# Sums for the modulation of a two-layer block: who makes them and when, on one Trainium2 core

## The reference, cut to what matters

```python
mod = jax.nn.silu(c) @ mod_w + mod_b
shift1, scale1, gate1, shift2, scale2, gate2 = [m[:, None, :] for m in jnp.split(mod, N_MOD, axis=-1)]
h = rms_norm(x, g_pre_mix) * (1 + scale1) + shift1
... # short convolution, stick-breaking attention, Mamba-2 scan, three gates, w_o
x = x + (gate1 * rms_norm(mix_out, g_post_mix)).astype(x.dtype)
h2 = rms_norm(x, g_pre_ffn) * (1 + scale2) + shift2
f = (jax.nn.silu(gt) * up) @ w_ffn_out
x = x + (gate2 * rms_norm(f, g_post_ffn)).astype(x.dtype)
```

## Time and profile before

| | before |
|---|---|
| median of 3 runs | 1602.61 us (1602.59 to 1605.82) |
| the profiled execution | 1604.25 us |
| its span, first to last instruction | 1602.5 us |
| mean granted clock of PE | 0.984 of full |
| busy: PE, DVE, ACT, POOL | 1531.8, 963.6, 672.4, 654.4 us |
| PE not busy in the span | 70.7 us |

### The profile page before, as it was taken

How to read it: one execution, slowest core, us unless ns; L and a number is a source line. 1 busy time by engine, 2 the same in 40 slices (tenths; PEclk the granted TensorE clock), 3 DMA queues, 4 the chain that set the end, 5 groups by cost and what they waited for, 6 DMA issues and landing times. The chain is left out here.

```text
span 1602.5 us, 23250 instructions
## 1 busy us (share of the span) xinstructions
PE 1531.8 (96%) x8908; PEld 1344.2 (84%) x8908; DVE 963.6 (60%) x1387; ACT 672.4 (42%) x1109; POOL 654.4 (41%) x535
## 2 busy tenths in 40 slices
PE   9999999989999999999999999199999999999998
PEld 8878887878888999988898887078888889999886
DVE  4342767447578777743568887045445888887423
ACT  6223444323544455422577673022225544445321
POOL 3871005741534222494206308888016356641000
PEclk9999999999999999999999999699999999999999
DMA  7532231423523333544231214335224234444331
GB/s 212 171 118 79 60 73 54 157 84 96 162 79 93 106 106 106 157 151 135 83 106 53 80 36 136 92 105 157 80 96 119 79 99 132 116 110 124 112 106 53
DMA packets 189620, 171.40 MB, mean 107 GB/s; under 512 B 20688, under 2 KB 162000, under 8 KB 189520
## 3 DMA queue, kind: packets, MB, share of 16 engines
q1 hardware_dynamic: 181456, 144.84, 30.3%
q0 software_dynamic: 8064, 25.20, 5.2%
HBM read 167.91 MB, written 2.10 MB: 106 GB/s over the span
## 5 line engine op out<-in xcount | busy, mean ns | idle before, releaser
L1566 DVE TENSOR_TENSOR w_lo<-raw,w_hi 128x2048 fp32r<-128x2048 f32 (+1 forms) x109 | 212.7, 1952 | 232.4 <-ACT w_hi L1084 232.3
L2275 PE MATMUL bank<-h_hi,w_hi 128*128 128x512 f32 (+1 forms) x800 | 310.0, 387 | 0.0
L2277 PE MATMUL bank<-h_hi,w_lo 128*128 128x512 f32 (+1 forms) x800 | 298.9, 374 | 0.0
L2276 PE MATMUL bank<-h_lo,w_hi 128*128 128x512 f32 (+1 forms) x800 | 298.7, 373 | 0.0
L1084 ACT CAST w_hi<-raw 128x2048 fp32r<-128x2048 f32 (+1 forms) x108 | 171.5, 1588 | 197.4 <-PE bank L2277 191.8
L951 POOL TENSOR_SCALAR mod_raw<-mod_raw,c_silu 128x512 f32<-128x512 f32 x96 | 193.2, 2012 | 21.7 <-DMA mod_raw<-in_mod_w 17.9
L2275 PEld LDWEIGHTS bank<-h_hi,w_hi 128*128 128x128 f32 x800 | 151.4, 189 | 29.3 <-issue 1.9
L2276 PEld LDWEIGHTS bank<-h_lo,w_hi 128*128 128x128 f32 x800 | 151.2, 189 | 27.2 <-issue 1.9
L2277 PEld LDWEIGHTS bank<-h_hi,w_lo 128*128 128x128 f32 x800 | 151.0, 189 | 27.4
L2369 PE MATMUL bank<-s_hi,w_hi 128*128 128x256 f32 x576 | 165.4, 287 | 8.7 <-DVE act_m L1808 6.9
L2370 PE MATMUL bank<-s_lo,w_hi 128*128 128x256 f32 x576 | 162.9, 283 | 0.0
(11 more groups left out here) (476 smaller groups left out, 3320.5 us busy)
## 6 DMA issues: line engine op xcount, KB each, us to landing
raw<-in_w_in SPq DMA_DIRECT2D x102, 512.0 KB, 4.6
mod_raw<-in_mod_w POOLq DMA_DIRECT2D x96, 256.0 KB, 3.1
raw<-in_w_ffn_in SPq DMA_DIRECT2D x44, 512.0 KB, 5.0
raw<-in_w_gate SPq DMA_DIRECT2D x22, 512.0 KB, 4.1
raw<-in_w_up SPq DMA_DIRECT2D x22, 512.0 KB, 5.3
raw<-in_w_down SPq DMA_DIRECT2D x20, 512.0 KB, 4.5
raw<-in_w_ffn_out SPq DMA_DIRECT2D x20, 512.0 KB, 4.4
raw<-in_w_out SPq DMA_DIRECT2D x8, 512.0 KB, 4.4
```

The source lines that it names most:

```text
L1566: ins = dve.tensor_tensor(w_lo[s][:, cols], raw[s][:, cols], w_hi[s][:, cols].bitcast(F32), ALU.subtract)
L2275: pe.matmul(o, st_hi, mv_hi, start=first, stop=False)
L2276: pe.matmul(o, st_hi, mv_lo, start=False, stop=False)
L2277: return pe.matmul(o, st_lo, mv_hi, start=False, stop=last)
```

## The change

1. **Four pairs by DVE in the first units.** Pairs 0, 1, 3 and 5 (`EARLY`) are summed beside q, k and va. GpSimd clears one of two accumulators (`mod_both`), loads the bias and issues slabs of 1 MB (256 rows by 1024 columns, 4 a pair, 16 in all) into two buffers that lie in `x_in`. DVE multiplies and adds in one instruction, `scalar_tensor_tensor` of 128x1024, two to a slab (`early_slab`). PE's `mod_columns` of the four stand behind the k units and inside the va units. gate2 (pair 5) becomes a column too; GpSimd later multiplies the identity by it, so that `mod_gate` can spread it.
2. **Two pairs stay** (`LATER`: 2 and 4) with GpSimd, unchanged in form (`mod_pair`). The steps of pairs 1, 3 and 5 vanish from GpSimd's order, and `mod_columns` from the end of up and from merge; the gains are scaled by one small DVE instruction (`scale_gain`).
3. **All input sums on DVE:** S3 moves from GpSimd to DVE, ahead of the first tile. The rests of the plain tiles (`tile_lo`) and `split(n0 + 3)` are put in another order on DVE and ACT.
4. **T3 by GpSimd,** with T2 and T4: `t3_part` leaves DVE, and GpSimd makes T3 as soon as the weights are in and p7 of the block before is done.

The core of the diff, first the places and GpSimd's part:

```diff
+        mod_both = [mod_raw, mod_acc]
+        mod_slabs = [at(f"mod_slabs{s}", A + 32 + 8 * s, [P, 2, 1024]) for s in range(2)]
+        EARLY, LATER = [0, 1, 3, 5], [2, 4]
+        SLABS = KD // 2
...
+            def early_pairs():
+                for e, pair in enumerate(EARLY):
+                    acc, col = mod_both[e % 2], 512 * MOD_PAIRS[pair][0]
+                    wait(gp, mod_read, e - 1)
+                    then(gp.memset(acc[:], 0.0))
+                    gp.dma_start(acc[0:1, :, :].rearrange("p a n -> p (a n)"), a["mod_b_2"][:, col:col + 1024]).then_inc(mod_b_in, 16)
+                    for d in range(SLABS):
+                        slab = SLABS * e + d
+                        wait(gp, mod_summed, slab - 1)
+                        gp.dma_start(mod_slabs[slab % 2][:], mod_w2[:, 2 * d:2 * d + 2, col:col + 1024]).then_inc(mod_w_in[slab % 2], 16)
...
-            def blocks(n0, which, c, pair, done):
-                s3 = s_sum[:, S3]
-                gp.wait_ge(h_lo_done, 2 * KD * (c + 1))
...
+            def blocks(n0, which):
                 for m in range(BLOCKS):
                     n = n0 + PLAIN + m
+                    t3, t2, t4 = four(operand(w_sum, n0, 2)), four(operand(w_sum, n0, 3)), four(t4_sum(n0, m))
+                    gp.wait_ge(raw_in[UNITS[n]["slot"]], UNITS[n]["raw"])
+                    wait_operand_free(gp, n0, which, m, 2)
+                    gp.tensor_tensor(t3, quarter_of(n, 1, 1), quarter_of(n, 0, 1), ALU.subtract).then_inc(block_pool, 1)
...
-                    if 1 <= m <= 2 * KD - done:
-                        mod_step(pair, done + m - 1)
             gp.wait_ge(c_ready, 1)
-            mod_pair(0)
+            gp.wait_ge(xn_b_ready, NT)
+            early_pairs()
+            gp.wait_ge(mod_read, 3)
...
-            mod_begin(1)
-            for i in range(9):
-                mod_step(1, i)
             for t in range(NT):
                 gp.wait_ge(var_ready, t + 1)
...
-            mod_begin(3)
-            for i in range(2):
-                mod_step(3, i)
             gp.wait_ge(ms2_ready, 1)
```

VectorE's part in the first units:

```diff
+            def early_slab(slab):
+                e, d = divmod(slab, SLABS)
+                acc = mod_both[e % 2][:].rearrange("p a n -> p (a n)")
+                dve.wait_ge(mod_w_in[slab % 2], 16 * (slab // 2 + 1))
...
+                then(dve.scalar_tensor_tensor(acc, parts[:, 0, :], c_silu[:, 2 * d:2 * d + 1], acc, ALU.mult, ALU.add))
+                dve.scalar_tensor_tensor(acc, parts[:, 1, :], c_silu[:, 2 * d + 1:2 * d + 2], acc, ALU.mult,
+                                         ALU.add).then_inc(mod_summed, 1)
...
+                if j == 3:
+                    early_slab(1)
+                    early_slab(2)
                 wait_full(dve, n_q + j, 1)
...
+                if j == 2:
+                    early_slab(0)
...
                 for j in range(2):
                     split(n_k + j + 1, pace)
+                    early_slab(3 + 4 * i + 2 * j)
+                    early_slab(4 + 4 * i + 2 * j)
+                    take(n_k + j, 1, k_t[:, 4 * i + 2 * j + 1, :], pace)
+                mod_columns(i, (shift_col[0], gain_sums[0])[i])
...
             split_rows(ra, c_rows)
+            early_slab(11)
             split(n_va + 2)
+            early_slab(12)
+            mod_columns(2, gain_sums[1])
+            early_slab(13)
+            early_slab(14)
             split(n_va + 1, chunk_pace(1))
-            mod_columns(0, shift_col[0], False)
+            early_slab(15)
             split(n_va + 2, chunk_pace(1))
+            mod_columns(3, gate_col)
```

VectorE's part in up and up2, and TensorE's in merge:

```diff
+                dve.wait_ge(h_lo_done, 2 * KD * (c + 1))
+                then(dve.tensor_tensor(s3, h_quarter(h_hi, 0, 0), h_quarter(h_hi, 1, 0), ALU.subtract))
+                then(dve.tensor_tensor(s3, s3, h_quarter(h_lo, 0, 0), ALU.add))
+                dve.tensor_tensor(s3, s3, h_quarter(h_lo, 1, 0), ALU.subtract).then_inc(block_dve, 1)
...
                     if m + 1 < BLOCKS:
                         t1_part(m + 1)
-                        t3_part(m + 1)
...
-            mod_columns(3)
-            branches(n_mg + 3, STILL, 4)
+            branches(n_mg + 3, STILL)
```

More of the change, by code:

```diff
@@ L662, in dve_order @@
                 yield from [f"m {m - 1}"] if m > 0 else []
-                yield from [f"t1 {ahead}", f"t3 {ahead}"] if ahead else []
+                yield from [f"t1 {ahead}"] if ahead else []
                 yield f"z {m}"
@@ L933, in mod_slab, with mod_pair @@
                 gp.dma_start(mod_raw[:, k % 2, :], mod_w[k, :, col:col + 512]).then_inc(mod_w_in[k % 2], 16)
-            def mod_begin(pair):
-                wait(gp, mod_read, pair)
+            def mod_pair(pair):
+                place = LATER.index(pair)
+                wait(gp, mod_read, len(EARLY) + place)
                 then(gp.memset(mod_acc[:], 0.0))
@@ L942, in mod_begin @@
                 mod_slab(pair, 0)
[L944 to L959, removed]
@@ L1008, in _ @@
                 gp.tensor_tensor(inv_rms[:, t:t + 1], var, power[:], ALU.pow).then_inc(ln_root, 1)
-            gp.wait_ge(merged, KD)
-            for i in range(9, 13):
-                mod_step(1, i)
             post_norm(0)
-            blocks(n_up, 0, 1, 1, 13)
+            blocks(n_up, 0)
             mod_pair(2)
@@ L1186, in hidden, with gate, tile_hi @@
             def hidden(n0, which):
-                def tile(n, m, j, pace):
-                    take(n, 0, silu_t[:, j, :], pace, ACT.Silu)
-                    wait_emptied(act, n, 1, pace)
-                    act.copy(m, bank[:, 4 + j, :]).then_inc(act_hi_done, 1)
+                def gate(n, j):
+                    if j == 1 and n == n0 + 3:
+                        act.wait_ge(act_lo_done, KF * which + 2)
+                    take(n, 0, silu_t[:, j, :], STILL, ACT.Silu)
+                def tile_hi(n, t, j):
+                    wait_emptied(act, n, 1)
+                    act.copy(act_hi[:, t, :], bank[:, 4 + j, :]).then_inc(act_hi_done, 1)
                 def pair_hi(m):
@@ L1851, in _ @@
             dve.tensor_tensor(wf_lo, wf_raw, wf_hi.bitcast(F32), ALU.subtract).then_inc(wf_split, 1)
-            with dve.Fori(0, 2) as i:
+            for i in range(2):
                 pace = pair_pace(i)
@@ L2534, in narrow, with mod_columns @@
                 ins.then_inc(row_mm, 1)
-            def mod_columns(pair):
-                pe.wait_ge(mod_summed, pair + 1)
+            def mod_columns(place):
+                early = place < len(EARLY)
+                acc = mod_both[place % 2] if early else mod_acc
+                pe.wait_ge(mod_summed, SLABS * (place + 1) if early else SLABS * len(EARLY) + 1)
+                wait(pe, mod_out, place if early else 0)
                 for q in range(KD):
                     cols = slice(P * (q % 4), P * (q % 4) + P)
-                    ins = pe.transpose(bank[:, 6 + q // 4, cols], mod_acc[:, q // 4, cols], ident[:])
+                    ins = pe.transpose(bank[:, 6 + q // 4, cols], acc[:, q // 4, cols], ident[:])
                 ins.then_inc(mod_read, 1)
@@ L2562, in _ @@
             f_pairs(n_q + 2, 1)
-            f_pairs(n_k, 2)
+            for i in range(2):
+                for j in range(2):
+                    for f in range(2):
+                        feature_tile(n_k + j, f, pair_pace(i))
+                mod_columns(i)
             pe.wait_ge(wf_split, 2)
```

168 lines of the change are left out of this document (89 added, 79 removed).

## The result

The changed kernel takes 1539.7 us (median of four, 1538.1 to 1540.4), the kernel before beside it 1603.8 (four, 1602.6 to 1605.8). The ratio is 0.9598, with a 95% interval from 0.9581 to 0.9614: 64 us are gone. I had predicted 1544, in a range from 1537 to 1558.

A forecast was written before the change was run, and what follows sets the result against it. TensorE bounds the kernel, busy 1531.8 of 1602.5 us, with one 37.6 us wait on GpSimd. Gains 40.3 + 4.9 + 8.4 + 7.4 - 2.0 = 59.0 from 1604.25 give 1545.2, median-adjusted to 1544, range 1537 to 1558.

The forecast's parts named there:

- Merge and norm: Merge's wait for pair 3 and Mamba's norm's wait for rr_diag: both go with their slow clock, gains 40.3 and 4.9 us.
- SGU: TensorE's wait for v_sgu: GpSimd idle at the roots, so wait and slow clock go, gain 8.4 us, bounds 0 and 8.4.
- The first units: Early slabs on VectorE beside q, k and va: no wait of TensorE, 0 us, bounds 0 and 6.
- VectorE's cover of 2.7 us a unit: First units: split, copy and two slabs fit a unit of 10.8 us with 2.7 us over.
- The slower rival: First units: two slabs in flight don't overlap, 12.4 us each, 1634 us; decides from 10.4 us a slab; chance 0.03.
- TensorE's own work: Transposes: three sets new in the first units, one leaves the end of up; 2.0 us lost, merge's counted separately.
- The blocks: Starts and blocks of up and up2: of 12.8 us of listed waits 5.4 stay, gain 7.4 us, bounds 12.8 and -7.8.
- The price of T3 on GpSimd: Blocks: GpSimd's T3 delays VectorE 0.65 us, so 0.1 us of wait in each of 34 blocks, 3.4 us.
- the first rival: Blocks: the port lock decides, each block waits 0.43 us, 14.6 us instead of 3.4, so 1555 us; chance 0.12.
- The two short waits: Rival: the waits for v_sgu and rr_diag stay, 13.3 us more, 1557 us; chance 0.08 including partial cases.
- Supply: Rival in the first units: slabs land late enough to delay split, costing 3 to 12 us, 1547 to 1556; chance 0.12.
- the DMA share in the first units: Sign in the first units: DMA share above 0.9, with no wait of TensorE.

The follow-up runs named there:

- The run with only the order changed: Kernel before, with GpSimd's nine steps of pair 1 moved behind the four roots of the SGU's norm: 1601.2 us, ratio 0.9984.
- the kernel with the pairs alone: Changed kernel with the start of the blocks and T3 as before the change, only the modulation pairs early: 1544.4 us.
- The run of the sums alone: Kernel before with S3 on VectorE, the new tile order and T3 on GpSimd, modulation pairs where they were: 1603.1 us, ratio 0.9997.
- the run with the useless sum: Changed kernel with T3 back on VectorE, plus GpSimd making the same difference into an unread buffer in up's 18 blocks: 1543.2 us.

## Why the prediction was right

**Merge and norm: right.** Forecast 40.3 + 4.9 = 45.2 us, measured 41.7 + 3.5 = 45.2 between the marks. That the merge has 1.4 more and the norm 1.4 less comes from the mark between them. In the trace of before, the six matmuls behind the norm's last one take from 993.50 to 996.15, 2.65 us, and in the changed kernel 1.46 (981.02 to 982.48). This is the slow clock behind the norm's wait, and 1.2 us of it lie behind the mark. Put back, the norm gives 4.7 and the merge 40.5. The run without pair 3's steps agrees: 40.8, less the same 1.2, and 0.9 more for the transposes that it keeps.

**SGU: right.** Forecast 8.4, measured 8.6 against the trace that the forecast was made from, and 6.5 to 7.9 against three other traces of the same code. The last tenths of this agreement are luck. The run with only the order changed shows what the trace of before could not: the wait can be had without moving the work to VectorE, but then 2.5 us are given back behind it.

**The first units: right.** Forecast 0 for slabs and sums, and three sets of transposes lost; measured 2.6 us for all of it. Without the slabs it is 0.7 us less, so the sum's zero holds, and the run with a third sum shows that VectorE's cover of 2.7 us a unit was not too high. The run with one slab in flight shows the edge: at 9.2 us a slab TensorE already loses 36 us. The slower rival's threshold of 10.4 us a slab fits this as an estimate: 16 x 1.2 us more would make 36 into 55, close to the 59 that I had for the gain.

**TensorE's own work: right.** Forecast -2.0; three sets more (-2.6 with all else in the first units) and one set of 1.03 us less at the end of up.

**The blocks: right in kind, mis-sized.** This is the term that missed. Forecast 7.4 us; measured 1.7 + (1.2 - 1.0) + 10.5 = 12.4. I priced waits as the list has them, 12.8 us before (13.3 with the two short ones for L1732 that the earlier trace rows leaves out), of which 5.4 would stay; 4.4 stayed, so the list explains 8.9. A listed wait is too short. TensorE's records in the kernel before around one of the 0.33 us:

```profile
1317.98 0.28 PE L2371 MATMUL bank<-h_hi,w_lo 128*128 128x256 f32 x1
1318.59 0.39 PE L2369 MATMUL bank<-s_hi,w_hi 128*128 128x256 f32 x1 [0.33 <-DVE act_m L1808]
1318.82 0.28 PE L2370 MATMUL bank<-s_lo,w_hi 128*128 128x256 f32 x1
```

Matmuls start 0.12 us apart and overlap. The one behind the wait starts 0.61 us after the last one, and the next only 0.23 after it. So a wait of 0.33 costs 0.49 + 0.11 = 0.60 us, 0.27 more than listed, and the distance of two such blocks, 1307.92 to 1318.59, is 10.67 instead of the steady 10.08, 0.59 more. Two other runs test this 0.27: the kernel with the pairs alone lists 6.8 us more in the blocks than the one with T3 on VectorE, in 8 more waits, 6.8 + 8 x 0.27 = 9.0, and takes 9.1 more. Of the 24 waits of before 6 remain: 18 x 0.27 = 4.9, and 8.9 + 4.9 = 13.8. The move of T3 costs some 2 us that stand in no list (4.9 between the marks, where two more waits of 2.4 in all give 2.9), which leaves 11.8, against the 12.4 measured. With 12.4 in place of 7.4 the forecast would have been 1538.6. It also stood on a median of before of 1602.6; the four runs have 1603.8, on which it would have been 1544.8, so that 1.2 us of the miss don't show.

Inside the term several of my reasons were off. The price of T3 on GpSimd was 3.4 us, and the run with T3 on VectorE measures 4.4; but I had it as 0.1 us of wait in each of 34 blocks, and it lies mostly at the two starts and in the first blocks of up, so that the size came near by luck. The 16 waits at 0.43 us, from which I took the bound of 14.6 for the first rival, are 13 with a step, most of 0.33. The bound was far too high with the steps gone. The run of the sums alone shows 14.2 us of waits with the steps in place, but in 19 waits and not 34, so the nearness means nothing. And the start was underrated: I had 2.0 us for each of the two, where the old and the new start differ by 9.1 us for both when T3 is on VectorE (1544.4 and 1535.3).

**The rivals.** T3 on GpSimd costs time in the blocks, 4.4 us and not 14.6. The two short waits went. Supply cost about 0.7 in the first units. Of the signs that I had named, the DMA share in the first units was 0.86 and not above 0.9, and L1833 is waited for in 6 pieces of 0.2 to 1.2 us, not by 0.1 in each block. What I had not seen is that the change carries one part, T3's move, that costs time: without it, 1535.3.

## What to carry to other kernels

A wait in the list costs what the distance of the same matmuls in two traces says, here 0.27 us more per wait than listed; with many short waits this is as large as the waits. A mark inside a slow stretch gives a part of one term to the next, so look at the matmuls on both sides of it. A wait that ends when GpSimd does can differ by 1.7 us between two executions of the same code; measure a stage against more than one trace of before. Work on GpSimd has two prices, its place in GpSimd's order and what it does to VectorE beside it: to reorder it paid 2 us here, to take it away 6.5 to 8.6, and two edits that both use GpSimd must be priced together (0.8 or nothing alone, 4.7 with the other). Before a step is moved behind a wait, look at what the engine did during that wait; the norm's two steps had filled 8 us that nobody else used, and to move them made the kernel 7 us slower.

## What the runs showed of the hardware

Of VectorE and GpSimd neither is always the one that is held. Where GpSimd's subtraction began 0.07 us behind VectorE's instruction in the changed kernel, it took 1.76 us, and the next VectorE instruction took 1.78. In the run with the useless sum it began 0.09 us behind in both kinds of block: in 9 it went the same way (1.74 and 1.78), in 5 three VectorE instructions in a row went ahead of it, 2.95 us, while they took 0.68 each. What decides between the two, no run shows. A GpSimd clear of 128x1024, which reads nothing, took 0.95 us, and left T1 beside it at 0.682 to 0.687. A load of 1 MB from GpSimd's queue took 5.9 us alone and 6.0, at most 7.8, with a second one behind it.
